# Engine lists of the FFN half reordered, and VectorE in place of GpSimd making the low parts of the down weights

## What is computed

```
h = rms_norm(x, norm_mix); z = h @ w_in            # q | k | v | u | gate logits
branch_a = window_attention(q, k, v, ...) @ w_attn_branch
branch_b = s5_mixer(u, ...) @ w_ssm_branch
x = x + (g_a * branch_a + g_b * branch_b) @ w_out
h = rms_norm(x, norm_ffn)
z = causal_dwconv(h @ w_up, conv_w, conv_b)        # 1024 -> 2 x 2816, depthwise width 3
val, gate = split(z); x = x + (gelu(gate) * val) @ w_down   # 2816 -> 1024
return rms_norm(x, norm_final)
```

## Time and profile before

| what | us |
|---|---|
| median of 3 runs | 2679.16 (2678.57 to 2680.88) |
| the profiled execution | 2677.93 |
| its span, first to last instruction | 2676.1 |
| PE busy | 2531.0 (95%) |
| DVE busy | 1528.4 (57%) |
| POOL busy | 959.4 (36%) |
| ACT busy | 729.3 (27%) |

### The profile page before, as it was taken

How to read it: one execution, slowest core, us unless ns; L and a number is a source line. 1 busy time by engine, 2 the same in 40 slices (tenths; PEclk the granted TensorE clock), 3 DMA queues, 4 the chain that set the end, 5 groups by cost and what they waited for, 6 DMA issues and landing times.

```text
span 2676.1 us, 34208 instructions
## 1 busy us (share of the span) xinstructions
PE 2531.0 (95%) x11906; PEld 2076.1 (78%) x11906; DVE 1528.4 (57%) x2209; ACT 729.3 (27%) x1413; POOL 959.4 (36%) x667
## 2 busy tenths in 40 slices
PE   4999999998999999797999999999989999999988
PEld 3787788886788888676878878888777888877877
DVE  7925355635788888426140235565458888883243
ACT  3125214212333333222121251142123333331111
POOL 1322222440233333474633222226103333336664
PEclk9999999998999999998999999999999999999999
DMA  5242342441122222544312123335211212125442
GB/s 182 94 102 85 134 142 95 142 173 55 57 85 84 80 86 94 212 162 141 133 55 94 53 99 136 117 111 177 109 48 72 93 73 91 76 89 212 141 173 102
DMA packets 117356, 298.53 MB, mean 112 GB/s; under 512 B 18136, under 2 KB 35320, under 8 KB 117256
## 3 DMA queue, kind: packets, MB, share of 16 engines
q1 hardware_dynamic: 78416, 217.22, 22.9%
q10 hardware_dynamic: 38840, 79.95, 8.5%
HBM read 228.45 MB, written 68.68 MB: 111 GB/s over the span
## 4 chain that ended last, share of the span: by engine, by line
PE 82%; DVE 11%; ACT 2%; DMA 2%; issue 2%; SPq 1%; POOL 0%; ACTq 0%; DVEq 0%; POOLq 0%
PE ps L414 25%; PE ps L416 25%; PE ps L415 25%; DMA act_hi<-ff 1%; DVE act_lo L1599 1%; DVE xres L1234 1%; PE ps L1940 1%; PE ps L1926 1%; DVE act_lo L1226 1%; PE ps L1875 1%; PE ps L1864 1%; PE ps L1791 1%; DVE slot_lo L1525 1%; PE ps L1943 1%; PE ps L1941 1%
## 5 line engine op out<-in xcount | busy, mean ns | idle before, releaser
L623 POOL CAST w_hi<-w_raw 128x1024 fp32r<-128x1024 f32 x72 | 78.7, 1093 | 747.9 <-PE ps L416 720.2
L666 POOL CAST slot_hi<-pair_raw 128x512 fp32r<-128x512 f32 x220 | 173.4, 792 | 478.7 <-PE ps L416 449.3
L414 PE MATMUL ps<-act_hi,w_hi 128*128 128x512 f32 x832 | 332.7, 400 | 8.6 <-DVE act_lo L1226 7.5
L416 PE MATMUL ps<-act_hi,w_lo 128*128 128x512 f32 x832 | 326.4, 392 | 0.0
L415 PE MATMUL ps<-act_lo,w_hi 128*128 128x512 f32 x832 | 325.6, 391 | 0.0
L414 PE MATMUL ps<-wd_hi,act_hi 128*128 128x512 f32 x704 | 278.9, 396 | 38.2 <-DVE act_lo L1599 38.2
L414 PE MATMUL ps<-act_hi,slot_hi 128*128 128x512 f32 x704 | 278.7, 396 | 14.8 <-DVE pre L1571 10.9
L415 PE MATMUL ps<-wd_lo,act_hi 128*128 128x512 f32 x704 | 277.6, 394 | 0.0
L415 PE MATMUL ps<-act_lo,slot_hi 128*128 128x512 f32 x704 | 277.3, 394 | 0.0
L416 PE MATMUL ps<-act_hi,slot_lo 128*128 128x512 f32 x704 | 277.2, 394 | 0.0
L416 PE MATMUL ps<-wd_hi,act_lo 128*128 128x512 f32 x704 | 276.9, 393 | 0.0
(11 more groups left out here) (319 smaller groups left out, 4903.8 us busy)
## 6 DMA issues: line engine op xcount, KB each, us to landing
w_raw<-in_wu SPq DMA_DIRECT2D x176, 512.0 KB, 3.4
pair_raw<-in_wu SPq DMA_DIRECT2D x88, 512.0 KB, 3.9
ff<-z SPq DMA_DIRECT2D x44, 512.0 KB, 2.6
act_hi<-ff SPq DMA_DIRECT2D x88, 256.0 KB, 3.6
gates<-junk ACTq DMA_DIRECT2D x64, 256.0 KB, 2.0
sig<-gates ACTq DMA_DIRECT2D x32, 512.0 KB, 5.2
tbl_o<-tables ACTq DMA_DIRECT2D x32, 384.0 KB, 3.4
tbl_r<-tables ACTq DMA_DIRECT2D x32, 256.0 KB, 2.7
```

Source lines behind the costliest of these rows:

```text
L414: nc.tensor.matmul(out, lh, rh, start=first, stop=False, skip_group_check=onto)
L416: return nc.tensor.matmul(out, ll, rh, start=False, stop=last, skip_group_check=onto)
L623: nc.gpsimd.tensor_copy(hi, w_raw[b][:, :]).then_inc(hi_made, 1)
L666: nc.gpsimd.tensor_copy(slot_hi[j][:, :, :], src).then_inc(slot_half[KIND[j]], 1)
```

## The change

No matmul, DMA or elementwise operation is added or taken away, but: from item 4 of the down product on, VectorE makes the low part of the weights (`weight_low`) and frees `w_raw`, and GpSimd keeps the high part; 40 items per block. The scaled last tile goes into a buffer of its own, `x_last`, so that `ffn_scaled` of it need not wait for its store; the wait is moved to `token_sum(2, 3)`. Operands 8 to 19 take a ring of four banks, with bank 2, in place of three, and p5 waits for operand 16. SyncE issues the loads of items 4 to 7 ahead of the 1 MB loads, and no longer waits for the last two stores before item 4. The rest is order: `operand_hi` and `operand_low` of 0 to 7 ahead of the second part of the norm; slots and weight sums between the token sums and operands; `c22` ahead of `down_low` at the end of the up loop, and the four `down_low` in two pairs; the next block's norm in two halves after items 16 and 18; the scaling of the finished tiles after item 25, with items 26 and 27 in between.

```diff
@@ operand_bank
-            return 4 + m % 4 if m < KD else 5 + (m - KD) % 3
+            if m < KD:
+                return 4 + m % 4
+            return (2, 5, 6, 7)[m % 4] if m < 20 else 5 + (m - 20) % 3
@@ sync
+                for b in range(2):
+                    sp.wait_ge(ff_st[b], 16 * ((blk + 1) * (FT // 2) - 1))
                 store_ff(blk, 0, FT - 2)
                 load_down(blk, 0, 2, 0)
                 load_down(blk, 0, 3, 0)
-                store_ff(blk, 0, FT - 1)
-                for b in range(2):
-                    sp.wait_ge(ff_st[b], 16 * (blk + 1) * (FT // 2))
                 for k in range(4, 8):
                     load_down(blk, 0, k, 0)
                     load_ff(blk, 0, k, 0)
                     if k == 5:
+                        store_ff(blk, 0, FT - 1)
+                    if k == 7:
+                        for b in range(2):
+                            sp.wait_ge(ff_st[b], 16 * (blk + 1) * (FT // 2))
                         sp.wait_ge(x2_st, 16 * TT * (blk + 1))
...
@@ gpsimd, down_item
+                    if isinstance(i, int):
+                        split(n_slot, n_all, b, wd[c % 4][0][:, :], wd[c % 4][1][:, :])
+                    else:
+                        pool.wait_ge(raw_in[b], n_slot * 16 + 16)
+                        pool.sem_inc(apart, 1)
+                        nc.gpsimd.tensor_copy(wd[c % 4][0][:, :], w_raw[b][:, :]).then_inc(hi_made, 1)
@@ scalar
                 ffn_root(0)
+                operand_hi(0, KD)
                 ffn_root(1)
-                operand_hi(0, KD)
...
-                with act.Fori(1, 5) as i:
+                with act.Fori(1, 4) as i:
                     for c in range(4):
                         down_hi(i, c)
...
-                for k in range(20, 23):
+                for k in range(16, 23):
                     down_hi(0, k)
+                    if blk + 1 < BLOCKS and k in (16, 18):
+                        x_squares(blk + 1, k // 2 - 8)
+                        x_root(blk + 1, k // 2 - 8)
@@ vector
+                def weight_low(i, c):
+                    n_all = i * 4 + (blk * UNITS + U_FFN + c)
+                    dve.wait_ge(hi_made, n_all + 1)
+                    tt(wd[c % 4][1][:, :], w_raw[c % 2][:, :], f(wd[c % 4][0][:, :]), ALU.subtract).then_inc(w_ready, 1)
+                    dve.wait_ge(w_ready, n_all + 1)
+                    dve.sem_inc(raw_free[c % 2], 1)
                 def down_low(i, c):
+                    if not isinstance(i, int) or c >= 4:
+                        weight_low(i, c)
...
                 residual(4, 6)
+                operand_low(0, KD)
                 ffn_scaled(1)
-                operand_low(0, KD)
...
                 residual(7, 8)
-                ffn_scaled(3)
-                for t in range(4):
-                    token_sum(t, 3)
                 slot_low(S3, 0, 0)
                 slot_low(S4, 0, 0)
+                ffn_scaled(3)
+                token_sum(0, 3)
+                token_sum(1, 3)
+                slot_low(W11, 0, 1)
+                token_sum(2, 3)
+                token_sum(3, 3)
+                slot_low(W12, 0, 1)
+                operand_low(8, 12)
                 slot_low(W22, 0, 0)
-                slot_low(W11, 0, 1)
-                slot_low(W12, 0, 1)
                 conv_row(0, 0)
-                for m in range(8, OPERANDS, 4):
-                    operand_low(m, m + 4)
+                operand_low(12, 16)
+                operand_low(16, 20)
+                weight_sum(S1, 0, 1)
+                operand_low(20, 24)
+                slot_low(S1, 0, 1)
+                weight_sum(S2, 0, 1)
+                operand_low(24, 28)
@@ vector, period: at the end of the loop
                     c11(i, c)
                     if not end:
                         slot_low(S2, i, c + 1)
+                    else:
+                        c22(i, c)
+                        down_low(0, 0)
+                        down_low(0, 1)
                     if not first:
                         ff_mul(i, c - 1)
...
                     c12(i, c)
                     if not end:
                         slot_low(S4, i, c + 1)
+                    else:
+                        down_low(0, 2)
+                        down_low(0, 3)
@@ vector, after the loop
-                with dve.Fori(1, 5) as i:
+                with dve.Fori(1, 4) as i:
...
-                for k in range(20, 23):
+                for k in range(16, 23):
                     down_low(0, k)
+                    if blk + 1 < BLOCKS and k in (16, 18):
+                        norm_x(blk + 1, k // 2 - 8)
...
                 down_low(0, 24)
-                out_norm(blk, 0, 4, out_parts(blk))
-                for k in range(25, 28):
-                    down_low(0, k)
+                down_low(0, 25)
+                out_root(blk, 0, 4, out_parts(blk))
+                out_scaled(0)
+                out_scaled(1)
+                down_low(0, 26)
+                out_scaled(2)
+                down_low(0, 27)
+                out_scaled(3)
```

More of the change, by code:

```diff
@@ L146, in build @@
         t2tok = at("t2tok", 136, [HK, HALF])
+        x_last = at("x_last", 164, [D])
         gffn = at("gffn", 132, [D])
@@ L1158, in _ @@
                 down_hi(0, 24)
+                down_hi(0, 25)
                 root(stat_o, var_o, std_o, out_parts(blk), 0, 4)
-                for k in range(25, 28):
-                    down_hi(0, k)
+                down_hi(0, 26)
+                down_hi(0, 27)
                 for i in range(4):
@@ L1227, in transposed_lo, with out_root @@
                         ALU.mult, ALU.subtract).then_inc(act_ready, 1)
-            def out_norm(blk, lo, hi, part):
+            def out_root(blk, lo, hi, part):
                 norm_scale(stat_o, lo, hi, sq_o, blk * TT + hi, var_o, std_o, part)
@@ L1232, in out_norm, with out_scaled @@
                     dve.wait_ge(gfin_in, 16 * (blk + 1))
+            def out_scaled(i):
+                stt(xres[:, i, :], xres[:, i, :], stat_o["rstd"][:, i:i + 1], gfin[:, :], ALU.mult, ALU.mult).then_inc(o_ready, 1)
+            def out_norm(blk, lo, hi, part):
+                out_root(blk, lo, hi, part)
                 for i in range(lo, hi):
-                    stt(xres[:, i, :], xres[:, i, :], stat_o["rstd"][:, i:i + 1], gfin[:, :], ALU.mult, ALU.mult).then_inc(o_ready, 1)
+                    out_scaled(i)
             def norm_x(blk, h):
@@ L1525, in slot_low, with late @@
                     tt(slot_lo[j][:, :, :], src, f(slot_hi[j][:, :, :]), ALU.subtract).then_inc(slot_ready[KIND[j]], 1)
+                def late(i):
+                    return xres[:, i, :] if i < TT - 1 else x_last[:, :]
                 def ffn_scaled(p):
@@ L1652, in period @@
                         slot_low(W22, i, c)
-                    if not end:
+                    if not end and not first:
                         weight_sum(S1, i, c + 1)
@@ L1672, in period @@
                         slot_low(W12, i, c + 2)
-                    if end:
-                        for k in range(4):
-                            down_low(0, k)
-                    if not first:
+                    if not first and not end:
                         c22(i, c)
@@ L1695, in _ @@
                 ff_mul(0, FT - 1)
-                with dve.Fori(1, 5) as i:
+                with dve.Fori(1, 4) as i:
                     for c in range(4):
                         down_low(i, c)
-                if blk + 1 < BLOCKS:
-                    for h in range(2):
-                        norm_x(blk + 1, h)
-                for k in range(20, 23):
+                for k in range(16, 23):
                     down_low(0, k)
+                    if blk + 1 < BLOCKS and k in (16, 18):
+                        norm_x(blk + 1, k // 2 - 8)
                 for i in range(3):
@@ L1784, in operands @@
                     if m >= 4:
[L1785 removed]
+                        pe.wait_ge(f_act, blk * OPERANDS + (m - 3 if m < 20 else m - 2))
                     for q in range(4):
@@ L1788, in operands @@
                         c2 = slice(HALF + k * P, HALF + (k + 1) * P)
-                        src = (xres[:, q, c], xres[:, q, c2], xres[:, q, c], t2tok[:, q, c], xres[:, HK + q, c2],
+                        src = (xres[:, q, c], xres[:, q, c2], xres[:, q, c], t2tok[:, q, c],
+                               xres[:, HK + q, c2] if q < HK - 1 else x_last[:, c2],
                                xres[:, HK + q, c], xres[:, q, c2])[kind]
```

26 lines of the change are left out of this document (12 added, 14 removed).

## The result

The changed kernel takes 2587.0 us (median of four runs, 2585.7 to 2587.9) where the one before takes 2679.3: a ratio of 0.9654 (0.9638 to 0.9671), 92.3 us less. The profiled execution took 2587.94 us, its span is 2586.2 us, 89.9 less than before.

What follows compares the result with a forecast made beforehand. PE, busy 95% of the span, was taken as the bound, leaving its idle and low-clock time. Opening 32, hand-over 16.6 and down product 29.3 sum to 77.9 us, giving 2602 us; own range 2592 to 2614, stated range 2588 to 2632.

Steps and rivals of the forecast that it cites:

- (a): FFN opening: operands 0 to 7 made ahead of the norm's second part end the low-part wait; gain 5.5 us per block.
- (b): FFN opening: with x_last the last token sum no longer waits for the store; gain 2.8 us, 0.7 left.
- (c): FFN opening, 3.9 us wait at tw_lo: moved slots and a fourth bank gain 2.8 us, plus about 1.1 of short waits.
- (d): FFN opening, first periods' waits of 1.9 and 1.2 us: VectorE's backlog moves into idle time; gain 3.1 us.
- (e): Up-to-down hand-over: c22 straight after c11 removes p4's wait and low clock; 7.0 us first block, 6.7 second.
- (f): Start of down product: items 6 and 7 load before the 1 MB loads, item 8 starves instead; gains 2.4 and 1.4 us.
- (h): Down product, item 25: its low part goes before the four scalings; waits of 7.9 and 7.8 us go, plus low clock.
- (g): Down product, before down_last: splitting the next block's norm over items 16 and 18 removes a 7.6 us wait, plus low clock.
- (i): Down product: moving 80 weight subtractions from GpSimd to VectorE is off the path in steady state; taken at nothing.
- (1): Rival: VectorE becomes late because it now gates raw_free and thus the loads; 2627 us, chance 0.24.
- (2): Rival: the 1 MB loads hurt less, nothing of the 11 us wait at item 8 stays; 2589 us, chance 0.05.
- (4): Rival: contention in the down product stretches VectorE's operations to 3.32 us each, making the kernel slower; 2699 us, chance 0.04.

Runs made afterwards that it cites:

- The doubled subtraction: Changed kernel with every down-weight subtraction on VectorE done twice, the second behind the first: 2595.2 us.
- the spread loads: Changed kernel with the 1 MB loads of residual and next block's x issued one behind each of items 8 to 15, x first: 2574.8 us.

## Why the prediction was right in kind and 15 us short

The step that failed is a term of the opening's sum, "0.7 for the short stretch at low clock" per block: it measured 4.0 and 4.5 us, 7.1 us more in all, where the table exceeds the forecast by 14.5. The other 7.4 are 1.9 of the openings' waits, 3.3 at items 2 to 8 and 2.2 elsewhere. A second step, the subtraction "taken at nothing", was wrong by itself and hardly moved the sum.

**The opening, 32 us forecast, 41 measured.** (a) Right: 5.5 us of wait, and the run without it lost 5.2 and 5.7 of spaces. (b) Right in size: 2.8 forecast, 2.7 and 3.5 of spaces in the run without it, with 0.9 us of wait left in the kernel after where I left 0.7. (c) and (d) were not undone alone; by the two traces the wait at `tw_lo` fell from 3.9 to 0.6 us, the 1.9 and 1.2 us at the first periods to 0 and 0.2. The waits together gave 15.5 us in the first block and 17.0 in the second, against the 15.3 of the sum. The term that failed is the last one, "0.7 for the short stretch at low clock": it measured 4.0 us in the first block and 4.5 in the second. The row was there: 0.95 over 130 us means, with levels of 1.2 and 2.4 GHz, 0.05 x 2 x 130 = 13 us at the lower one, so at most 6.5 us lost; 4.0 were, since a part of the 13 us fell into PE's waits. I had turned p4's 5.29 us into a price for the hand-over but not this row. In the first block PE did some 27 transposes and eight matmuls at that level, a transpose every 0.21 us instead of 0.11. The opening's own upper bound of 17 was too low for the same reason. The 9 us are most of the 15.

**The hand-over.** (e) Right by place, 7.2 and 7.2 us against 7.0 and 6.7. The 0.5 us for items 2 and 3 was not paid; neither waits. (f) Right in mechanism: the starved item is 8, with 9.27 us of wait where I had 11 and the same low clock behind it. The failed term is the time from the issue of the 1 MB loads to the next weights: 26.65 us measured, 28.8 carried over from before; with SyncE's list taken back it is again 29.2 (1083.33 to 1112.52). Why it is shorter in the new order isn't shown. Wrong in kind was to price (e) and (f) as two sums. (e) is worth 0.6 us in the first block once the queue decides, and (f) 6.7 and 7.0 once PE is early, both from one trace each.

**Inside the down product.** Right in size by place, 30.8 us against 29.3, and half right in cause: the lists do it without the subtraction (2589.5 us), but at item 25 the subtraction does it without the lists. (h) was credited with both waits at item 25, 19.7 us with their low clock; undone alone it costs nothing. (g) was credited with 9.6; undone it costs 3.8 to 5.3, though the split alone takes the whole 10.7. (i) was put at nothing; alone it gives 27 us. What saved the forecast is that the two causes replace each other, and each wait can be removed only once; I had not seen that, and for (i) the sum came out by luck.

**The rivals.** (1) didn't happen: no wait of VectorE's making is longer than before. The doubled subtraction shows that it begins within the first 1.2 us more per item, at the three places named there, and nowhere else. (2) named 2589, near the result, for the wrong reason: the wait at item 8 didn't go. My argument against it, "the time is bytes, not order", is refuted by the spread loads: the same bytes in another order, and no wait. (3) is excluded by the table, (4) by VectorE's subtractions, which take 1244 ns on the mean; none of the 80 made PE wait in steady state. The casts of GpSimd, which VectorE now meets with two-source operations of its own, took 1115 ns on the mean of all 80, and 1127 on that of all 88 in the kernel before. One premise of my case against (4) was wrong: the subtraction that held `ff_mul` up in the earlier trace rows is one of items 0 to 3, which stay on GpSimd.

**What stays open.** The medians and the stretches of one trace differ by some us for three runs (the list of SyncE: 9.4 against 13.7; the hand-over: 8.1 against 6.6; the norm: 3.8 against 5.3), since the start of the program and of the second block vary by 2 to 4 us from one execution to the next. The worth of a single step is known to about 3 us, not better. That (c) and (d) gave what the traces show is read, not tested.

## What to carry to other kernels

Price the low clock of a stretch by its granted clock, not by the one wait that you have taken apart: 130 us at 0.95 held 4.0 us of it, the one wait at the hand-over 2.6. When a change holds two edits that shorten the same wait, one by hiding a slow operation and one by making it fast, the gain by place says nothing about either; undo each and both. A transfer of many MB that is needed late goes behind the small ones that are needed soon, one at a time: 12 us for a few lines here.

## What the runs showed of the hardware that I had not expected

- A scaling of 128x1024 with two large sources takes VectorE 2742 ns while GpSimd subtracts weights and 1473 ns while it only casts them, a low part of 128x512 1178 and 737 ns. A product of 128x4 elements takes 0.16 us alone and 1.94 us when it begins 0.5 us after a subtraction of GpSimd: it ends when that ends. Taking 80 subtractions away from GpSimd and giving them to VectorE made the work that VectorE already had so much shorter that it is busy for only 32 us more instead of 99.
- In the opening a single wait of PE of 3.6 to 5.5 us cost 0.9 to 1.6 us more by the lower clock level behind it; the waits of the opening in the kernel before (three long ones, 2.8 to 5.5 us in the first block) cost 4.0 and 4.5 together. The 4.1 us wait at the hand-over cost 1.8 (6.0 less 4.2 of spaces).
- The DMA engines moved 305 GB/s over 60 us with PE, VectorE and GpSimd at work, and PE was busy for all of it at clock 1.00.
